# Sums of squares in array quadrants, two tiles at once, and modulation units gathered in rows of one PSUM region

## The chip, the cores and the metric

The kernel runs on one core of one Trainium2 chip, in one launch. The metric is the device time of an execution in microseconds; the lower, the better. TensorE is called PE here, ScalarE ACT, VectorE DVE, GpSimd POOL and SyncE SP.

## What is computed

A stack of three mixer blocks over 512 tokens of width 1024, all in float32. What matters here, cut from the reference:

```python
def _rms(x, gain):
    xf = x.astype(jnp.float32)
    return xf * lax.rsqrt(jnp.mean(xf * xf, axis=-1, keepdims=True) + EPS) * gain.astype(jnp.float32)

def _l2norm(x):
    return x * lax.rsqrt(jnp.sum(x * x, axis=-1, keepdims=True) + EPS)
...
        mod = c_act @ w_ada[layer] + b_ada[layer]          # 1024 -> 3072, for two layers
        shift, scale, gate = mod[:, :D], mod[:, D:2 * D], mod[:, 2 * D:]
...
            mkv = c_act @ w_ada_kv + b_ada_kv              # 1024 -> 2048
...
    q = _l2norm(qkv[..., :W].reshape(B, T, H, Dh)) * (Dh ** -0.5)      # first mixer (GDN), 8 heads of 128
    k = _l2norm(qkv[..., W:2 * W].reshape(B, T, H, Dh))
...
    q = _rms(proj[..., :W].reshape(B, T, H, Dh), q_gain).transpose(0, 2, 1, 3)   # second mixer, 16 heads of 64
...
        q = rms_norm(q.reshape(B, S, N_ATTN_HEADS, HEAD_DIM), q_norm_w) * HEAD_DIM ** -0.5   # third, 24 heads of 64
        k = rms_norm(k.reshape(B, S, N_ATTN_HEADS, HEAD_DIM), k_norm_w)
```

The queries and keys of all three mixers are normalised by the length of each head's vector (128 numbers in the first mixer, 64 in the others), and the modulation is a vector times a matrix, 8192 columns in all.

## The kernel before

Activations lie transposed: the width on the 128 partitions, the 512 tokens along the free axis. One tile is 128 x 512 and holds one head of 128 or two heads of 64. The large products run in blocks of 512 weight columns, two units each (`dense_unit`). ACT splits the raw weights into a high part (`split_hi`, L596), POOL subtracts it to get the low part (`split_lo`, L463), and PE does three products of the parts, 24 matmuls of 512 columns for one tile (L1587). The weights come by SP in loads of 1 MB into two slots of `raw` (L394), freed by POOL's subtraction. Each engine's program is written out by hand in the order in which it runs; semaphores are all that ties the engines together.

**Sums of squares.** For the length of a head ACT squares a tile into one of four `work4` buffers (`square`, L601), and PE multiplies it by a 128 x 128 matrix of ones, `ones` for a head of 128 and `onesbd` (two 64 x 64 blocks of ones) for two heads of 64 (`sums`, L1681). So each of 128 PSUM partitions gets its own head's sum. ACT turns it into a factor in two operations, a Ln out of PSUM (L624) and an Exp in place (L626), in `root`; there are two buffers `rbuf` and two banks, 4 and 5 (`ssbank`). DVE multiplies the tile by the factor (L1145 in GDN, `gained`, L1324, elsewhere) and frees the buffer. PE puts the sums between dense work of the next block: `gdn_sums` in the blocks D_Z and D_Z + 1 of the GDN stage (16 tiles), `head_sums` and `later_sums` elsewhere (40 tiles: KB, QB, QA2, KA2, QB2, KB2, two tiles at a time, with one dense tile between the two pairs that share a unit).

**Modulation units.** The 8192 columns of the modulation are 32 units of 256. A unit is eight matmuls (L1670): the stationary is one column of `cact` repeated 32 times, the moving operand 128 x 256 weights, and four strips of 32 output partitions, k % 4, take the products. The first eight units run at the start. The other 24 are fillers in the first mixer's inverse, one at the head of each pair of heads and one in each of its five levels. DVE copies each unit's row out of PSUM into `arow` (`ada_row`, L1080), and before the next unit PE turns it into two columns of 128 in `modps` with two matmuls of one column (`ada_columns`, L1654). At the end DVE adds the biases (L1239).

**A level of the inverse.** For two heads, PE does 2 x 8 matmuls of 64 x 64 (L1816), a filler, then 2 x 16 more (L1829, L1831). DVE merges the first product into `yib` in between (`copy_predicated`, L1229), ACT copies the rest out (L741, L743), POOL restores a buffer (L480).

```python
                    for s in range(2):
                        ...
                            last = mm(block64(3 * s + 1, i, c), ntm[rs, s, i, :], xin[rs, s, i, :],
                                      start=True, stop=True)
                        last.then_inc(y_full, 1)
                    filler()
                    for s in range(2):
                        ...
                        pe.wait_ge(yi_done, n)
```

**Other places.** The attention of the second mixer has matmuls on row halves (L1960: 64 of the 128 rows, all columns) and on column halves (L1995: all rows, 64 columns), and the scan's first products lie on opposite quadrants (L1879). V tiles of the third mixer are copied by ACT (`v_tile`, L949) and moved into place by SP (`v_moves`, L414); the z values of the first two mixers are silu's that ACT takes from PSUM (L685 and L686, L874).

## Time and profile before

| What | us |
|---|---|
| median of 3 runs | 1387.74 (1384.92 to 1388.86) |
| the profiled execution | 1383.2 |
| its span, first to last instruction | 1381.2 |
| PE busy | 1277.0 |
| ACT busy | 551.5 |
| DVE busy | 462.0 |
| POOL busy | 392.1 |
| mean granted clock of PE | 0.959 of full |

The time of an execution is a little more than the span of its instructions, 2.0 us in the profiled one. Busy times add up the instructions of an engine; an engine that is busy for most of the span is a candidate for the bound, and a stage is bound by the engine that others wait for there. In the timelines a float32 matmul shows as two records, so a row "x4" is two matmuls; its start is exact, and its end overlaps the start of the next, so costs are read from start to start. The times in brackets are how long the engine had been idle and who released it.

### The profile page before, as it was taken

Reading aid. Unit: us, or ns where it says so; the run is one execution under the profiler, and the core shown is the slowest. Engines: PE = TensorE matmul, PEld = TensorE weight load, DVE = VectorE, ACT = ScalarE, POOL = GpSimd, SP = SyncE. Lnnn points to the kernel's source line nnn. Section 1 sums busy time; section 2 is a strip of 40 time slices with the busy share of each in tenths; the row PEclk is TensorE's granted clock in tenths of the full one; section 3 lists DMA queues with packets and bytes.
Section 4 is the critical chain, followed back from the end, with each engine's and each line's share of the span. In section 5 each row is a group of like instructions: output and inputs, shape, how many; then the busy total and the mean of one; then the engine's idle time right before and its main releaser. Section 6 shows DMA issues by size and latency. Waiting matters only on the chain.

```text
span 1381.2 us, 20140 instructions
## 1 busy us (share of the span) xinstructions
PE 1277.0 (92%) x8386; PEld 976.4 (71%) x8386; DVE 462.0 (33%) x852; ACT 551.5 (40%) x926; POOL 392.1 (28%) x170
## 2 busy tenths in 40 slices
PE   5699999889989798999997887989999999999979
PEld 3488876677878676777774554867887777777647
DVE  0665533333234314242213334130202332323441
ACT  4244348522224423343345774233233433644400
POOL 0244432222234331333440001224143222335131
PEclk9799999999999899999999999999999999998969
DMA  9533321155550111222222000132132321224001
GB/s 302 155 92 91 91 92 61 50 167 168 171 185 1 62 61 61 92 91 92 82 77 63 19 20 31 62 97 89 34 107 92 99 69 62 72 85 172 9 0 61
DMA packets 106571, 120.48 MB, mean 87 GB/s; under 512 B 5072, under 2 KB 92528, under 8 KB 106488
## 3 DMA queue, kind: packets, MB, share of 16 engines
q1 hardware_dynamic: 102224, 114.83, 26.0%
q10 hardware_dynamic: 4264, 4.45, 1.1%
q8 instruction: 63, 1.03, 0.3%
q14 instruction: 20, 0.16, 0.0%
HBM read 111.41 MB, written 2.10 MB: 82 GB/s over the span
## 4 chain that ended last, share of the span: by engine, by line
PE 82%; ACT 8%; DVE 4%; issue 3%; DMA 2%; SPq 1%; ACTq 0%; POOL 0%; DVEq 0%
PE ps L1587 47%; PE ps L1681 4%; PE ps L2120 3%; PE ps L1960 2%; PE ps L1670 2%; PE ps L1831 2%; PE ps L1977 2%; PE ps L1829 2%; PE ps L1995 1%; PE ps L2089 1%; PE ps L1902 1%; PE ps L2076 1%; PE ps L1897 1%; PE ps L1816 1%; PE ps L2036 1%
## 5 line engine op out<-in xcount | busy, mean ns | idle before, releaser
L463 POOL TENSOR_TENSOR wlo<-raw,whi 128x2048 fp32r<-128x2048 f32 x58 | 266.6, 4597 | 685.0 <-ACT whi L596 541.1
L596 ACT ACTIVATE whi<-raw 128x2048 fp32r<-128x2048 f32 x56 | 106.9, 1911 | 268.9 <-PE ps L1587 234.3
L1681 PE MATMUL ps<-work,cs 128*128 128x512 f32 x160 | 77.9, 607 | 4.3 <-ACT work L601 4.1
L624 ACT ACTIVATE rbuf<-ps,cs 128x512 f32<-128x512 f32 x59 | 40.0, 678 | 63.7 <-PE ps L1681 49.0
L471 POOL TENSOR_TENSOR wlo<-raw,whi 128x2048 fp32r<-128x2048 f32 x10 | 46.2, 4621 | 66.9 <-ACT whi L660 66.9
L983 ACT ACTIVATE p<-sc,nmx 128x256 f32<-128x256 f32 x64 | 32.0, 502 | 59.0 <-DVE nmx L1428 59.0
L1587 PE MATMUL ps<-hC_hi,whi 128*128 128x512 f32 x208 | 55.3, 408 | 0.0
L1587 PE MATMUL ps<-hC_lo,whi 128*128 128x512 f32 x208 | 51.4, 389 | 0.0
L1587 PE MATMUL ps<-hC_hi,wlo 128*128 128x512 f32 x208 | 51.4, 389 | 0.0
L660 ACT ACTIVATE whi<-raw 128x2048 fp32r<-128x2048 f32 x12 | 23.0, 1920 | 68.7 <-PE ps L1587 63.4
L1681 PEld LDWEIGHTS ps<-work,cs 128*128 128x128 f32 x160 | 29.6, 192 | 29.1 <-issue 17.3
L1359 DVE SCALAR_TENSOR_TENSOR nlk<-ps,att 128x768 f32<-128x768 f32 x16 | 15.3, 958 | 98.1 <-ACT att L896 98.1
L1587 PEld LDWEIGHTS ps<-hC_hi,whi 128*128 128x128 f32 x208 | 38.9, 188 | 12.2 <-issue 4.6
L1977 PE MATMUL ps<-nlk,cs 128*128 128x128 f32 (+3 forms) x128 | 44.8, 453 | 1.7 <-DVE nlk L1359 1.7
L1587 PEld LDWEIGHTS ps<-hC_lo,whi 128*128 128x128 f32 x208 | 39.0, 188 | 8.3
L1587 PEld LDWEIGHTS ps<-hC_hi,wlo 128*128 128x128 f32 x208 | 39.0, 188 | 8.1
L1428 DVE CUSTOM_DVE_ANT_0 sc<-ps,biast 128x256 f32<-128x256 f32 (+1 forms) x64 | 23.6, 398 | 62.6 <-PE ps L2067 32.9
L1587 PE MATMUL ps<-hA_hi,whi 128*128 128x512 f32 x176 | 43.5, 389 | 0.0
L1587 PE MATMUL ps<-hA_lo,whi 128*128 128x512 f32 x176 | 43.5, 389 | 0.0
L1587 PE MATMUL ps<-hA_hi,wlo 128*128 128x512 f32 x176 | 43.5, 389 | 0.0
L741 ACT ACTIVATE xin<-ps 128x128 f32<-128x128 f32 x32 | 9.0, 281 | 84.9 <-PE ps L1831 84.9
L1960 PE MATMUL ps<-qTb,kTb 64*128 64x512 f32 (+1 forms) x64 | 27.4, 551 | 15.7 <-ACT att L900 12.7
(369 smaller groups left out, 2867.9 us busy)
## 6 DMA issues: line engine op xcount, KB each, us to landing
raw<-in_w_in_dram SPq DMA_DIRECT2D x24, 1024.0 KB, 5.1
raw<-in_w_in_a_dram SPq DMA_DIRECT2D x16, 1024.0 KB, 5.5
raw<-in_w_ada_dram SPq DMA_DIRECT2D x16, 1024.0 KB, 5.1
raw<-in_w_ada_kv_dram SPq DMA_DIRECT2D x8, 1024.0 KB, 5.3
raw<-in_w_kv_dram SPq DMA_DIRECT2D x8, 1024.0 KB, 5.2
raw<-in_w_in_b_dram SPq DMA_DIRECT2D x8, 1024.0 KB, 5.2
ada_a<-in_w_ada_dram SPq DMA_DIRECT2D x4, 1024.0 KB, 9.1
ada_b<-in_w_ada_dram SPq DMA_DIRECT2D x4, 1024.0 KB, 12.6
```

What stands on the lines that cost most here:

```text
L463: pool.tensor_tensor(wlo[:, s, :], raw[:, s, :], whi[:, s, :].bitcast(F32), ALU.subtract).then_inc(lo_ready, 1)
L471: pool.tensor_tensor(wlo[:, s, :], raw[:, s, :], whi[:, s, :].bitcast(F32), ALU.subtract).then_inc(lo_ready, 1)
L596: A(whi[:, s, :], raw[:, s, :], ACT.Copy).then_inc(hi_ready, 1)
L624: A(rbuf[:, g % 2, :], ssbank(g), ACT.Ln, scale=1.0 / width, bias=epsc).then_inc(ss_read, 1)
L983: A(p2[:, n % 2, 256 * e:256 * e + 256], sc2[:, n % 2, 256 * e:256 * e + 256], ACT.Exp, scale=-1.0, bias=nmx[:, grp, t, 2 * hp + e:2 * hp ...
L1587: last = mm(out, l[a], r[b], start=start and at == 0, stop=stop and at == n - 1)
L1670: last = mm(modrow(u)[32 * (k % 4):32 * (k % 4) + 32, :], cact[:, k:k + 1].broadcast_to([128, 32]), src[:, k, :], start=k < 4, stop=k >= 4)
L1681: mm(ssbank(g), stat, work4[:, n % 4, :], start=first, stop=last).then_inc(sq_used, 1)
L1829: mm(block64(3 * s + 2, i, c), XT[rs, h, i, :], yib[rs, s, lv % 2, i, :], start=True, stop=True)
L1960: last = mm(logit_cols(s, off[j], 512 - 128 * j), k, q, start=j != 3, stop=True, skip_group_check=True)
L1977: last = mm(logit_cols(s, off[j], width), C("negtri"), nlk[s][:, off[j]:off[j] + width], start=False, stop=True, skip_group_check=True)
L2120: last = mm(dense[2 * s + m], w[:, k, 128 * m:128 * m + 128], x[:, k, :], start=q == 0, stop=q == 23)
```

## The change

It does four things.

1. `head_sums` takes two tiles together. Each is summed in two matmuls of a 64 x 64 block of ones: the first tile's halves go to their own partitions, the second tile's halves to each other's. The four matmuls use the four quadrants of the array, in the order up-up, up-down, down-down, down-up (rows used, then partitions written).
2. `gdn_sums` takes two tiles together as well, with 128 x 64 ones: one tile's sum is written to partitions 0 to 63 and the other's to 64 to 127 of one bank (`gdn_bank`).
3. On ACT `root_pair` and `root_halves` take the place of two calls of `root`. The first has three Ln (the second tile's halves are put back to their partitions) and two Exp; the second has one Ln for both tiles and four Exp on 64 partitions, two for each tile, since both halves of its 128 partitions need the same sums.
4. The 24 later modulation units no longer use a repeated column: the stationary is a window of 32 columns of `cactz`, zero but for one column, so that unit n adds only to row n of each strip, and all 24 gather in one PSUM region. One copy by DVE and two matmuls (`late_columns`) turn all of them into columns at the end; `ada_columns` and `ada_row` are gone from the loop. POOL builds `cactz` once.

```diff
+                cactz = sb("cactz", [128, KD, 55], F32, s2)
...
+        def gdn_bank(g):
+            return ps[:, 4 + (g - G_GDN) // 2 % 2, :]
...
+            pool.wait_ge(hlo_ready, KD)
+            pool.memset(cactz[:, :, :], 0.0).then_inc(cz_done, 1)
+            pool.wait_ge(cz_done, 1)
+            pool.wait_ge(cact_ready, 1)
+            pool.tensor_copy(cactz[:, :, 23:24], cact[:, :].unsqueeze(2)).then_inc(cz_done, 1)
...
+            def root_pair(g, summed):
+
+                act.wait_ge(sq_used, summed)
+                r_used(g - 1)
+                first, second = rbuf[:, g % 2, :], rbuf[:, (g + 1) % 2, :]
+                A(first, ssbank(g), ACT.Ln, scale=1.0 / 64, bias=epsc).then_inc(ss_read, 1)
+                A(second[0:64, :], ssbank(g + 1)[64:128, :], ACT.Ln, scale=1.0 / 64, bias=epsc[64:128, :])
+                A(second[64:128, :], ssbank(g + 1)[0:64, :], ACT.Ln, scale=1.0 / 64, bias=epsc[0:64, :]).then_inc(ss_read, 1)
+                act.wait_ge(ss_read, g + 1)
+                A(first, first, ACT.Exp, scale=-0.5).then_inc(r_ready, 1)
+                act.wait_ge(ss_read, g + 2)
+                A(second, second, ACT.Exp, scale=-0.5).then_inc(r_ready, 1)
+
+            def root_halves(g, summed):
+
+                act.wait_ge(sq_used, summed)
+                r_used(g - 1)
+                first, second = rbuf[:, g % 2, :], rbuf[:, (g + 1) % 2, :]
+                A(second, gdn_bank(g), ACT.Ln, bias=epsc).then_inc(ss_read, 2)
+                act.wait_ge(ss_read, g + 2)
+                A(first[64:128, :], second[0:64, :], ACT.Exp, scale=-0.5)
+                A(first[0:64, :], second[0:64, :], ACT.Exp, scale=-0.5).then_inc(r_ready, 1)
+                act.wait_ge(r_ready, g + 1)
+                A(second[0:64, :], second[64:128, :], ACT.Exp, scale=-0.5).then_inc(rh_read, 1)
+                act.wait_ge(rh_read, (g - G_GDN) // 2 + 1)
+                A(second[64:128, :], second[64:128, :], ACT.Exp, scale=-0.5).then_inc(r_ready, 1)
...
-                for t in range(t0, t0 + 4):
-                    root(G_GDN + t, SQ_GDN + t + 1, 1)
+                for t in (t0, t0 + 2):
+                    root_halves(G_GDN + t, SQ_GDN + t + 2)
...
-                filler_row()
...
-                    filler_row()
-
-
-            while rows_left:
-                ada_row(rows_left.pop(0))
-            dve.wait_ge(mod_full, 32)
-            TT(mods[:, 16:64], modps[:, 16:64], cols1[:, 40:88], ALU.add).then_inc(mods_ready, 1)
+
+            dve.wait_ge(ada_done, 32)
+            copy(arow[:, 0, :], modrow(2 * EARLY)).then_inc(row_done, 1)
+            dve.wait_ge(mod_full, 2 * EARLY + 1)
+            TT(mods[:, 16:64].rearrange("p (u m) -> p m u", m=2), modps[:, 16:64].rearrange("p (m u) -> p m u", m=2),
+               cols1[:, 40:88].rearrange("p (u m) -> p m u", m=2), ALU.add).then_inc(mods_ready, 1)
...
+            def late_columns():
+
+                pe.wait_ge(row_done, 2 * EARLY + 1)
+                for m in range(2):
+                    last = mm(modps[:, 16 + 24 * m:40 + 24 * m], arow[:, 0, 128 * m:128 * m + 128], C("sel32"),
+                              start=True, stop=True)
+                last.then_inc(mod_full, 1)
+
+            def late_unit(a, s):
+
+                n = 2 * (a - EARLY) + s
+                pe.wait_ge(raw_loaded[s], 16 * (load_of["ada", a] + 1))
+                if n == 0:
+                    pe.wait_ge(cz_done, 2)
+                for k in range(KD):
+                    last = mm(modrow(2 * EARLY)[32 * (k % 4):32 * (k % 4) + 32, :], cactz[:, k, 23 - n:55 - n],
+                              raw_ch(s)[:, k, :], start=n == 0 and k < 4, stop=n == 23 and k >= 4, skip_group_check=True)
+                last.then_inc(ada_done, 1)
...
-            def head_sums(n0, g0):
-                for j in range(2):
-                    sums(n0 + j, g0 + j, onesbd)
+            def head_sums(n, g):
+
+                pe.wait_ge(sq_ready, n + 2)
+                pe.wait_ge(ss_read, g)
+                up, down = slice(0, 64), slice(64, 128)
+                for tile, of, to in ((0, up, up), (1, up, down), (0, down, down), (1, down, up)):
+                    last = mm(ssbank(g + tile)[to, :], ones[of, 0:64], work4[of, (n + tile) % 4, :], start=True, stop=True)
+                last.then_inc(sq_used, 2)
...
             def gdn_sums(*tiles):
-                for t in tiles:
-                    sums(SQ_GDN + t, G_GDN + t, ones)
+                if not tiles:
+                    return
+                n, g = SQ_GDN + tiles[0], G_GDN + tiles[0]
+                pe.wait_ge(sq_ready, n + 2)
+                if tiles[0] >= 4:
+                    pe.wait_ge(ss_read, g - 2)
+                for k in range(2):
+                    last = mm(gdn_bank(g)[64 * k:64 * k + 64, :], ones[:, 0:64], work4[:, (n + k) % 4, :],
+                              start=True, stop=True)
+                last.then_inc(sq_used, 2)
```

The order moves in three kinds of place; all the dense work stays where it was.

PE, one level of the inverse of the first pair of heads, before (xin and ntm are the level's operands, cs and arow the constants and the row that is turned, raw and cact the weights and the activated vector):

```order
L1816 MATMUL ps<-xin,ntm 64x64 x16
L1654 MATMUL ps<-cs,arow 128x1 x2
L1670 MATMUL ps<-raw,cact 32x256 x8
L1829 MATMUL ps<-yib,xa 64x64
L1831 MATMUL ps<-xa,yib 64x64
```

and in the changed kernel:

```order
L1874 MATMUL ps<-xin,ntm 64x64 x16
L1705 MATMUL ps<-raw,cactz 32x256 x8
L1887 MATMUL ps<-yib,xa 64x64
L1889 MATMUL ps<-xa,yib 64x64
```

The two matmuls of one column are gone; the eight of the unit now stand right behind the sixteen of the level.

PE, the first two pairs of head sums (tiles KB of the keys, in the blocks D_KB + 1), before:

```order
L1587 MATMUL ps<-hk_hi,wlo 128x512 x8
L1681 MATMUL ps<-work,cs 128x512 x2
L1587 MATMUL ps<-hk_hi,whi 128x512 x8
L1587 MATMUL ps<-hk_lo,whi 128x512 x8
L1587 MATMUL ps<-hk_hi,wlo 128x512 x8
L1681 MATMUL ps<-work,cs 128x512 x2
```

and in the changed kernel:

```order
L1619 MATMUL ps<-hk_hi,wlo 128x512 x8
L1738 MATMUL ps<-work,cs 64x512 x4
L1619 MATMUL ps<-hk_hi,whi 128x512 x8
L1619 MATMUL ps<-hk_lo,whi 128x512 x8
L1619 MATMUL ps<-hk_hi,wlo 128x512 x8
L1738 MATMUL ps<-work,cs 64x512 x4
```

Two matmuls of 128 columns of weights became four of 64, at the same places.

ACT, the first pair of roots of the KB tiles, before:

```order
L601 ACTIVATE work<-kTb 128x512 x2
L596 ACTIVATE whi<-raw 128x2048
L624 ACTIVATE rbuf<-ps,cs 128x512
L626 ACTIVATE rbuf<-rbuf 128x512
L624 ACTIVATE rbuf<-ps,cs 128x512
L626 ACTIVATE rbuf<-rbuf 128x512
```

and in the changed kernel:

```order
L614 ACTIVATE work<-kTb 128x512 x2
L609 ACTIVATE whi<-raw 128x2048
L646 ACTIVATE rbuf<-ps,cs 128x512
L647 ACTIVATE rbuf<-ps,cs 64x512
L648 ACTIVATE rbuf<-ps,cs 64x512
L650 ACTIVATE rbuf<-rbuf 128x512
L652 ACTIVATE rbuf<-rbuf 128x512
```

Ln and Exp used to alternate; now three Ln stand ahead of two Exp. In GDN the first pair of roots is, in the changed kernel:

```order
L614 ACTIVATE work<-qkvT 128x512 x4
L659 ACTIVATE rbuf<-ps,cs 128x512
L661 ACTIVATE rbuf<-rbuf 64x512
L662 ACTIVATE rbuf<-rbuf 64x512
L664 ACTIVATE rbuf<-rbuf 64x512
L666 ACTIVATE rbuf<-rbuf 64x512
```

where before stood:

```order
L601 ACTIVATE work<-qkvT 128x512 x4
L624 ACTIVATE rbuf<-ps,cs 128x512
L626 ACTIVATE rbuf<-rbuf 128x512
L624 ACTIVATE rbuf<-ps,cs 128x512
L626 ACTIVATE rbuf<-rbuf 128x512
```

One Ln and four Exp on 64 partitions are in the place of two Ln and two Exp.

## Rows read from the trace of the kernel before

**Rows 1.** The page: busy time by engine; granted clock and DMA rate in 40 slices

```profile
PE 1277.0 (92%) x8386; PEld 976.4 (71%) x8386; DVE 462.0 (33%) x852; ACT 551.5 (40%) x926; POOL 392.1 (28%) x170
...
PEclk9799999999999899999999999999999999998969
...
GB/s 302 155 92 91 91 92 61 50 167 168 171 185 1 62 61 61 92 91 92 82 77 63 19 20 31 62 97 89 34 107 92 99 69 62 72 85 172 9 0 61
```

**Rows 2.** The page: shares of the chain of waits by engine

```profile
PE 82%; ACT 8%; DVE 4%; issue 3%; DMA 2%; SPq 1%; ACTq 0%; POOL 0%; DVEq 0%
```

**Rows 3.** Timeline of PE, 1177 to 1186 (start, duration, line, operation, records)

```profile
1177.26 1.88 PE L1681 MATMUL ps<-work,cs 128*128 128x512 f32 x4
...
1182.65 1.98 PE L1587 MATMUL ps<-hC_hi,wlo 128*128 128x512 f32 x8
1184.46 1.88 PE L1681 MATMUL ps<-work,cs 128*128 128x512 f32 x4
```

**Rows 4.** Timeline of PE in the attention, 799 to 804

```profile
799.58 2.37 PE L1995 MATMUL ps<-att,Vb 128*64 128x512 f32 x16
801.88 0.69 PE L1960 MATMUL ps<-qTb,kTb 64*128 64x512 f32 x1
...
803.37 0.40 PE L1963 MATMUL ps<-bandbf 128*128 128x128 bf16 x4
```

**Rows 5.** Timeline of PE, one level of the inverse, 280 to 286

```profile
280.90 1.43 PE L1816 MATMUL ps<-xin,ntm 64*64 64x64 f32 x32
282.26 0.61 PE L1654 MATMUL ps<-cs,arow 128*128 128x1 f32 x4
282.79 1.07 PE L1670 MATMUL ps<-raw,cact 128*32 128x256 f32 x16
283.79 0.34 PE L1829 MATMUL ps<-yib,xa 64*64 64x64 f32 x4
...
285.71 1.43 PE L1816 MATMUL ps<-xin,ntm 64*64 64x64 f32 x32
```

**Rows 6.** Timeline of PE, start of the scan

```profile
411.30 1.96 PE L1879 MATMUL ps<-V,xa 64*64 64x128 f32 x32 [0.39 <-DVE mods L1239]
```

**Rows 7.** Timeline of ACT in the GDN stage, roots and z values

```profile
219.95 0.69 ACT L624 ACTIVATE rbuf<-ps,cs 128x512 f32<-128x512 f32 x1 [1.03 <-DVE qkvT L1145]
...
221.20 0.67 ACT L624 ACTIVATE rbuf<-ps,cs 128x512 f32<-128x512 f32 x1
...
223.85 0.59 ACT L685 ACTIVATE zs<-ps 64x512 f32<-64x512 f32 x1
```

**Rows 8.** Timeline of ACT, first gate values of the z block

```profile
703.07 1.57 ACT L874 ACTIVATE zsT<-ps 128x512 f32<-128x512 f32 x3
```

**Rows 9.** Tile vB, its moves and their landing; timeline of PE there

```profile
L414 SPq DMA_DIRECT2D vB<-yst x8: 594/596/1290, 1258.4 to 1263.7; - x8
...
DMA to landing us min/median/max: 2.0/2.1/3.1
...
1266.44 1.12 PE L2089 MATMUL ps<-pT,vB 128*64 128x128 f32 x8
```

**Rows 10.** Timeline of PE at 306; windows (busy us, count; clock, DMA share, GB/s)

```profile
306.12 0.68 PE L1816 MATMUL ps<-xin,ntm 64*64 64x64 f32 x16 [1.25 <-DVE xin L1222]
...
297.50:320.00 22.50, 19.90 (x384) 17.08 (x383) 9.83 (x29) 7.35 (x24) 4.12 (x6) 0.92 0.42 132
```

**Rows 11.** Timeline of DVE in the level of rows 5

```profile
282.37 0.29 DVE L1229 COPY_PREDICATED yib<-cs,ps 128x128 f32<-128x128 int32 x1 [0.46 <-PE ps L1816]
```

**Rows 12.** Timelines of PE and ACT, the waits of the GDN stage

```profile
214.20 1.98 PE L1681 MATMUL ps<-work,cs 128*128 128x512 f32 x4 [1.37 <-ACT work L601]
...
232.52 1.98 PE L1681 MATMUL ps<-work,cs 128*128 128x512 f32 x4
...
231.84 2.19 ACT L601 ACTIVATE work<-qkvT 128x512 f32<-128x512 f32 x4
...
257.45 1.16 PE L1789 MATMUL ps<-cs,gt 128*128 128x128 f32 x8 [0.42 <-ACT zs L686]
```

More of the change, by code:

```diff
@@ L67, in constants @@
     put("first32", p % 32 == 0)
+    put("sel32", p % 32 == np.arange(24)[None, :])
     def dft(n):
@@ L830, in row_squares, with roots @@
                         square(sq + j, src(j))
-            def roots(g, sq, js=range(4)):
+            def roots(g, sq, js=(0, 2)):
                 for j in js:
-                    root(g + j, sq + j + 1, 64)
+                    root_pair(g + j, sq + j + 2)
             def copies(d, dst, done, func):
@@ L1763, in filler @@
                 if fill:
-                    ada_unit(*fill.pop(0))
+                    late_unit(*fill.pop(0))
             for p in range(HG // 2):
```

31 lines of the change are left out of this document (12 added, 19 removed).

## The prediction

> **What bounds the kernel now.** I read the page first, by engine and by slice: TensorE (PE) is busy 92% of the 1381.2 us, and the granted clock is close to full nearly everywhere [rows 1]. The chain that ended last lies 82% on PE [rows 2]. So a microsecond taken off PE is a microsecond of the span wherever PE has no waits, and nothing where it waits. Hence the order of views: the timeline of PE around each place that the change touches, then the timelines of ACT, DVE and the SP queue at the same moments, to see who would be late next.
>
> **The change, part by part.**
>
> *Head sums (20 pairs of tiles: KB 4, QB 4, QA2 2, KA2 2, QB2 4, KB2 4).* Today a pair is two matmuls with a 128x128 stationary and 512 columns (each is two records in the trace). From the start of one pair to that of the next there are 7.20 us, with one dense tile between [rows 3]. That tile is 24 matmuls, three groups of 8, and the last group takes 1.81 us (1184.46 less 1182.65), so 5.44 us in all. A pair costs 7.20 - 5.44 = 1.76 us, 0.88 us for one matmul. Afterwards a pair is four 64x64 matmuls of 512 columns, one in each quadrant of the array. Before has no four quadrants at once, so bounds: not under 0.88 us, since each still streams 512 columns; 1.76 us if they run two at a time; 3.5 us if one at a time. The nearest rows are these. In the attention, 16 records (8 matmuls, 2560 columns, alternating between two column halves) run from 799.58 to 801.88, that is 2.30 us where 2560 columns at 0.88 per 512 would take 4.40 [rows 4]: two of 512 columns at once cost 0.92 us. In the modulation units eight matmuls of 256 columns in four column strips take 1.00 us [rows 5] where one after another would take 3.52. Ideal would be 0.88, so 0.12 us is for weights and for leaving and entering the shape. Rows and columns of the array can therefore be shared by neighbours: strips share all rows, and matmuls on the two row halves, which share all columns, take 1.49 us for 1280 columns (801.88 to 803.37; 2.20 one by one) [rows 4]. I take 1.00 us for a pair: 0.76 saved, 20 times, 15.2 us.
>
> The Trainium skill (PSUM — Partial Sum Buffer, section on bank collisions) says that different row tiles cannot access the same PSUM bank at the same time. Here both halves of a bank are written from different row halves, so by that rule at most two of the four would overlap. The trace leans the other way: 32 records (16 matmuls of 128 columns) whose neighbours sit on opposite row halves and write opposite halves of one bank take 1.96 us, where 16 x 128 columns at 0.88 per 512 would be 3.52 [rows 6]. They overlap, in one bank. By the rule the 15.2 us would be about nothing; it stays a rival.
>
> What covers the ACT side. root_pair has five ACT operations for four, the two new ones on 64 partitions, and 64 partitions cost as much as 128 (0.59 us, [rows 7]). But the two Ln of the second tile now stand between a Ln and its Exp, and fill the bubble there; a pair goes from 2 x 1.25 us [rows 7] to some 2.7. In the dense stages ACT idles 3 us and more before each pair (3.60 us is the usual), so 0.2 us is hidden; without that idle it would be 4 us over 20 pairs. Two places give something back. Behind the last pair of QB, ACT's first gate value of the z block is done at 703.07 + 0.60 = 703.7 [rows 8], and PE, one dense tile behind that pair, comes to its bank at 704.8; PE will be 1.5 us earlier there: -0.3. Behind the last pair of KB2 the V tiles are copied by ACT and moved by SP (32 DMAs of 0.6 us). The last is issued at 1263.7 and lands 2.1 us later, 1265.8, and PE's first weighted sum starts at 1266.44 [rows 9]. The start of these moves hangs on ACT's last pair, whose start is set by DVE's use of the roots before it, which a subtraction on POOL holds up. So they don't get earlier, and of PE's last 1.5 us only some 0.3 remain: -1.2. Head sums: 15.2 - 0.3 - 1.2 = **13.7 us**.
>
> *Modulation units.* Between the levels of the inverse, PE does a filler: two matmuls that turn the previous row into columns (L1654), then eight for the next unit (L1670). In the steady pattern L1816 starts at 280.90, L1654 at 282.26, L1670 at 282.79, L1829 at 283.79, L1816 again at 285.71 [rows 5]: no wait, a period of 4.81 us of which L1654 takes 0.53. The change removes it 23 times, and keeps one pair at the end. Three of the 23 stand at the head of a later pair of heads, ahead of a 1.25 us wait for DVE [rows 10]: worth nothing, since DVE's chain does not shorten. The other 20 are worth 0.53 each, one of them 0.95 (the first level of all, at the low clock): **11.0 us**. Who is late next? L1829 waits for DVE's merge, which ends 0.40 us after L1816 (282.37 + 0.29 = 282.66, [rows 11]); the eight matmuls left, 1.00 us, still cover it. If they did not, up to 0.4 us a level would be lost. The stationary of a unit is now 32 different columns instead of one repeated, at the same shape; I cost that at nothing. The 24 copies of rows on DVE (0.42 us each) go too; DVE was not the bound. The loads of 1 MB are still released by the units; a period of 4.28 us asks for 245 GB/s instead of 218, and the first slice of the page shows 302 [rows 1], so I expect no wait. POOL's new memset and copy fall in a 21 us idle stretch of POOL.
>
> *GDN sums (8 pairs).* On PE the same gain, 0.76 x 8 = 6.1 us. But ACT sets the pace here. PE waits 1.37 us for ACT's squares at 214.20, finds them just ready at 232.52, and waits 0.42 us for zs at 257.45 [rows 12]. root_halves has one Ln and four Exp on 64 partitions, three of them chained by semaphores: about 0.72 + 0.55 + 3 x 0.62 = 3.1 us, for 2.5 [rows 7]. And PE now waits for both squares of a pair, 0.54 us more. At the first wait: ACT 0.1 later and both squares needed, so PE starts its pair 0.7 later and finishes it as before. By the second wait ACT has done two longer pairs, so its squares (231.84) start 1.1 later, PE begins at 234.1 instead of 232.52 and is 0.8 us behind. Three more pairs make it 1.5 ahead, but then ACT's last pair is 0.6 longer, and the zs values come only some 0.2 us earlier. PE just waits longer at 257.45. GDN: **0.2 us**, between -3 (ACT's 8 x 0.6 all on the path, less what PE gains at the ends) and +1.5.
>
> Sum: 13.7 + 11.0 + 0.2 = 24.9 us. The profiled execution took 1383.2 us, so it would be 1358.3. The median of the runs is 4.5 us above it, 1387.7, so the forecast is **1362.8 us**.
>
> **Rivals.**
> A. *Two quadrants at a time* (the PSUM rule above, or a limit of another kind on four streams). A pair costs 1.76 + 0.12 = 1.9 us, the head sums lose 2.8 us, and the total is 11.0 + 0.2 - 2.8 = 8.4: 1379.3 us. For it: no row shows four quadrants. Against it: rows 6, and the four strips of rows 5. Chance 0.12.
> B. *Quadrants that share a row or a column half do not overlap.* In the order issued (up-up, up-down, down-down, down-up) each neighbour shares a side, so all four run one by one: 3.5 + 0.1 = 3.6 us, 1.84 more than now, 20 times, 36.8 us on a bound PE. Total +36.8 - 11.0 - 0.2 = +25.6: 1413.3 us, slower. It decides as soon as a pair costs over 2.3 us. Against it: strips share rows, row halves share columns, and both overlap [rows 4, 5]; but none does it at 64x64. Chance 0.06.
> C. *The levels do not get shorter.* With less work between DVE's waits the clock stays low for longer: today it is 0.92 over 297.5 to 320 us, which holds such a start [rows 10], and the first level there runs at half rate. Were one more level at half rate in each of the four head pairs (about 2.4 us each), or were the DMAs to set the period, most of the 11 us would go: 1373 us. Chance 0.10.
> That the two parts do not do what they say is covered by A and B for the sums. For the units the instructions removed are plain in the order.
>
> **How the numbers follow.** Forecast 0.70 (1358 to 1370: pair cost 0.88 to 1.2, GDN -3 to +1.5, levels 9 to 12), A 0.12, B 0.06, C 0.10, and 0.02 for about no change by waits that I have not seen. The range takes in C and reaches to A: 1358 to 1378. About 0.3% (4 us) is what a measurement can tell from no change, and A and C are past that too: faster 0.70 + 0.12 + 0.10, less 0.02 for their edge, 0.90; same 0.04; slower 0.06.
>
> **What would show it.** A pair of head sums at about 1.0 us, 6.4 us from one to the next in the KB2 stage; under 0.9 or over 1.3 the sizing is wrong, at 1.9 it is A, at 3.6 B. No 128x1 matmuls in the levels, and a period of 4.28 us; a wait on DVE before the 64x64 matmuls behind the filler, or on the raw loads, would be C. In GDN longer waits of PE for the squares at about 212 and 232 us and for zs at about 256. A wait of about 1 us before the first weighted sum of the second window, on the V moves. If the head stages shrink by less than 12 us while the pair costs 1.0, ACT's five operations were not hidden after all.

## The result, and the profile after

The changed kernel took **1367.1 us** (median of 4 runs, 1365.0 to 1371.8), the kernel before beside it 1388.0: ratio 0.986, 95% interval 0.983 to 0.989. That is 20.9 us less, where 24.9 was forecast and 1362.8 us named. The profiled execution of the change is its slowest, 1371.8 us with a span of 1369.7; the one of before was among its fastest, 1383.2. In a later comparison (e9 below), the change took 1367.7 against 1388.4.

The page after, lines that answer to [rows 1, 2]. The shares of the chain add up to 82% here and to 100% before: as the view follows it, this chain begins only at 236 us, so 68% does not mean that PE counts for less.

```profile
PE 1257.0 (92%) x8374; PEld 950.5 (69%) x8374; DVE 439.5 (32%) x829; ACT 570.0 (42%) x954; POOL 393.8 (29%) x172
...
PEclk9799998999999899999998999999999999999969
...
GB/s 302 160 93 92 92 92 33 55 163 193 179 186 1 62 62 61 93 92 93 92 98 34 20 20 4 77 84 89 62 94 78 129 41 87 66 88 181 9 1 62
```

```profile
PE 68%; ACT 8%; issue 3%; DVE 3%; POOL 0%; DMA 0%; SPq 0%; ACTq 0%; DVEq 0%
```

PE is 20 us less busy and just as full in proportion; ACT is 18 us busier (570.0 for 551.5). So in most places the time went with PE's work, as it should where PE is the bound. The slices of the page are too coarse to say where not. I cut both traces at the first product of each stage in PE's timeline instead:

| stage (from, to: first product of) | before | after |
|---|---|---|
| start to the first GDN sum | 200.38 | 199.42 |
| GDN sums, to the first head of the inverse (L1789, now L1847) | 57.07 | 62.53 |
| inverse, with the modulation units, to the scan | 153.85 | 143.44 |
| scan, first part (to the first transposed output) | 26.09 | 26.09 |
| rest of the scan, KB and QB (8 pairs of head sums) | 292.87 | 289.87 |
| attention, to the first product of the third mixer's wfs | 212.76 | 216.99 |
| QA2 and KA2 (4 pairs) | 140.36 | 138.69 |
| first window, QB2 and KB2 (8 pairs) | 177.05 | 173.10 |
| second window | 58.38 | 57.06 |
| end, to PE's last product | 59.19 | 59.39 |

The inverse gave what was forecast, the head sums two thirds of it, and GDN lost 5.5 us where 0.2 were to be gained. Three views show how.

**A pair of head sums.** PE's timeline in KB of the changed kernel (start, duration, line, operation, records), which answers to [rows 3]:

```profile
564.72 1.09 PE L1738 MATMUL ps<-work,cs 64*64 64x512 f32 x8
565.74 2.11 PE L1619 MATMUL ps<-hk_hi,whi 128*128 128x512 f32 x8
567.69 1.99 PE L1619 MATMUL ps<-hk_lo,whi 128*128 128x512 f32 x8
569.52 1.98 PE L1619 MATMUL ps<-hk_hi,wlo 128*128 128x512 f32 x8
571.42 1.09 PE L1738 MATMUL ps<-work,cs 64*64 64x512 f32 x8
```

From its own start to that of the next work a pair takes 1.02 us (565.74 less 564.72): four quadrants do run at once. But the next pair starts 6.70 us later, not 6.4. The dense tile in between takes 5.68 and not the 5.44 of three groups at 1.81: its first group takes 1.95 and its last 1.90, the middle one 1.83. By the forecast's own sum a pair costs 6.70 - 5.44 = **1.26 us**.

The pair's 1.02 us must not be set against the same cut in the kernel before. There, in the period of [rows 3],

```profile
1178.57 2.42 PE L1587 MATMUL ps<-hC_hi,whi 128*128 128x512 f32 x8
```

follows 1.31 us behind the start of the pair (1177.26), and the dense tile then takes 5.89. The first dense record starts 0.03 us after the last record of the sums, though one such record takes 0.43. So part of the sums' time lies behind that start, and only whole periods, 7.20 and 6.70, can be compared.

**A level of the inverse**, in PE's timeline, which answers to [rows 5]:

```profile
314.00 1.44 PE L1874 MATMUL ps<-xin,ntm 64*64 64x64 f32 x32
315.37 1.07 PE L1705 MATMUL ps<-raw,cactz 128*32 128x256 f32 x16
316.37 0.34 PE L1887 MATMUL ps<-yib,xa 64*64 64x64 f32 x4
...
318.28 1.43 PE L1874 MATMUL ps<-xin,ntm 64*64 64x64 f32 x32
```

The period is 4.28 us, and nothing waits for DVE.

**The GDN sums**, in PE's timeline, which answer to [rows 12]; in brackets how long PE stood idle and for whom:

```profile
209.39 1.07 PE L1619 MATMUL ps<-whi,hA_lo 128*128 128x512 f32 x4
214.54 1.98 PE L1788 MATMUL ps<-work,cs 128*64 128x512 f32 x4 [4.08 <-ACT work L614]
216.44 2.08 PE L1619 MATMUL ps<-whi,hA_hi 128*128 128x512 f32 x4
...
220.98 1.08 PE L1788 MATMUL ps<-work,cs 128*64 128x512 f32 x4
...
236.11 1.21 PE L1788 MATMUL ps<-work,cs 128*64 128x512 f32 x4 [1.96 <-ACT work L614]
```

The wait of 1.37 us has become 4.08, and one of 1.96 is new; both stand where the forecast had longer waits, and are longer than it had them. What follows the waits is slow: the pair at 214.54 takes 1.90 us to the next start where the one at 220.98 takes 1.01. The window of this stage, of both kernels (busy PE and count, granted clock, DMA share, GB/s), first after:

```profile
199.42:261.95 62.53, 54.84 (x221) 0.92 0.11 37
```

In the kernel before, with the other engines' busy time ahead of the clock (PE, PEld, DVE, ACT, POOL):

```profile
200.38:257.45 57.07, 55.28 (x222) 37.10 (x220) 15.17 (x29) 43.46 (x73) 10.31 (x6) 1.00 0.13 41
```

The clock was full all through before. Now it falls to its lower level, 1.2 GHz, at both idles: 0.51 of full from 212.9 to 219.9, 0.52 from 236.8 to 240.3, and 1.00 in the rest of the stage. ACT's own timeline shows what comes ahead of the squares:

```profile
200.59 0.69 ACT L659 ACTIVATE rbuf<-ps,cs 128x512 f32<-128x512 f32 x1 [4.14 <-issue]
201.31 0.63 ACT L661 ACTIVATE rbuf<-rbuf 64x512 f32<-64x512 f32 x1
...
203.28 0.63 ACT L666 ACTIVATE rbuf<-rbuf 64x512 f32<-64x512 f32 x1
208.19 0.69 ACT L659 ACTIVATE rbuf<-ps,cs 128x512 f32<-128x512 f32 x1 [4.29 <-DVE qkvT L1185]
...
213.35 2.17 ACT L614 ACTIVATE work<-qkvT 128x512 f32<-128x512 f32 x4
```

A pair of roots takes 3.3 us (200.59 to 203.91) instead of 2.5. The second pair waits 4.29 us for DVE to use the first roots, and DVE stands at its copy of the gate products (L1179), which wait for PE. Only then come the split and the squares for which PE waits at 214.54. That wait is not new. The kernel before has it at the same place, and longer:

```profile
209.23 0.69 ACT L624 ACTIVATE rbuf<-ps,cs 128x512 f32<-128x512 f32 x1 [5.21 <-DVE qkvT L1145]
...
213.53 2.17 ACT L601 ACTIVATE work<-qkvT 128x512 f32<-128x512 f32 x4
```

What the change did to it shows when times are counted from the first GDN sum (200.38 before, 199.42 after), before and after: DVE's copy starts at 7.48 and 6.78, ACT's second roots at 8.85 and 8.77, its squares at 13.15 and 13.93, PE's pair at 13.82 and 15.12. The copy comes 0.70 us earlier, since PE gained that much, but the roots gain next to nothing from it: a pair of them needs both buffers back, so it waits for two scalings of DVE (0.6 us each) where one was enough. Then the roots take 0.8 longer, and PE waits for two squares and not one. PE itself is there 1.4 us earlier, and that too is in the 4.08.

### The profile page after: what moved, and what is told of

The parts are those of the page before. It is cut to its first block, busy times and chain, and to the rows that moved or that the text cites. A ratio compares the mean times of both kernels' runs of the same rounds, so it can differ in the third digit from the quotient of the medians.

```text
span 1369.7 us, 20045 instructions
## 1 busy us (share of the span) xinstructions
PE 1257.0 (92%) x8374; PEld 950.5 (69%) x8374; DVE 439.5 (32%) x829; ACT 570.0 (42%) x954; POOL 393.8 (29%) x172
## 4 chain that ended last, share of the span: by engine, by line
PE 68%; ACT 8%; issue 3%; DVE 3%; POOL 0%; DMA 0%; SPq 0%; ACTq 0%; DVEq 0%
PE ps L1619 36%; PE ps L2178 3%; PE ps L2035 2%; PE ps L2018 2%; PE ps L1705 2%; PE ps L1889 2%; PE ps L1887 1%; PE ps L2053 1%; PE ps L1738 1%; PE ps L1960 1%; PE ps L2147 1%; PE ps L1955 1%; PE ps L1874 1%; PE ps L2094 1%; PE ps L2134 1%
## 5 line engine op out<-in xcount | busy, mean ns | idle before, releaser
L2035 PE MATMUL ps<-nlk,cs 128*128 128x128 f32 (+3 forms) x128 | 48.5, 485 | 2.8 <-DVE nlk L1391 2.8
L1328 DVE SCALAR_TENSOR_TENSOR xT<-ps,mods,xT 128x512 f32<-128x512 f32 x16 | 12.0, 751 | 89.7 <-PE ps L1619 89.7
L2018 PE MATMUL ps<-qTb,kTb 64*128 64x512 f32 (+1 forms) x64 | 26.0, 528 | 15.6 <-ACT att L940 12.6
L1874 PE MATMUL ps<-xin,ntm 64*64 64x64 f32 x640 | 27.8, 224 | 13.4 <-DVE xin L1256 11.9
L1889 PE MATMUL ps<-xa,yib 64*64 64x64 f32 x640 | 38.8, 226 | 0.0
```

What stands on the lines that cost most here:

```text
L1889: last = mm(block64(3 * s, i, c), yib[rs, s, lv % 2, i, :], XT[rs, h, i, :], start=True, stop=True)
L2018: last = mm(logit_cols(s, off[j], 512 - 128 * j), k, q, start=j != 3, stop=True, skip_group_check=True)
L2035: last = mm(logit_cols(s, off[j], width), C("negtri"), nlk[s][:, off[j]:off[j] + width], start=False, stop=True, skip_group_check=True)
```

## The experiments

Twelve runs, in three groups (e1 to e4, e5 to e8, e9 to e12), each group beside the kernel before on one chip; the medians of the kernel before there are 1387.3, 1385.7 and 1388.4 us. Three things were open: how the three parts add up, why GDN loses, and why a pair costs 1.26 us.

### The parts one by one: e1, e2, e3, e4

Each kernel is the change with some parts put back as before. e1 keeps the modulation units alone, e2 the head sums, e3 the GDN sums, e4 both head sums and units. Against the change, e4 is:

```diff
-                for t in (t0, t0 + 2):
-                    root_halves(G_GDN + t, SQ_GDN + t + 2)
+                for t in range(t0, t0 + 4):
+                    root(G_GDN + t, SQ_GDN + t + 1, 1)
...
-                for k in range(2):
-                    last = mm(gdn_bank(g)[64 * k:64 * k + 64, :], ones[:, 0:64], work4[:, (n + k) % 4, :],
-                              start=True, stop=True)
-                last.then_inc(sq_used, 2)
+                for t in tiles:
+                    sums(SQ_GDN + t, G_GDN + t, ones)
```

> The modulation part of the change alone; head and GDN sums of squares as before. Theory (the parts are independent, the term was right): in the profile of the changed kernel a level repeats every 4.28 us, where before it was 4.81, and the stretch from the first inverse to the scan was 10.4 us shorter. So 10 to 11 us under the kernel before, about 1377.5, with a level period of 4.28 us and the scan's start 10 us earlier. Rival (the levels were shorter only because another part of the change helped, or part of the gain is given back by the attention): 4 to 8 us.

> The four-quadrant head sums alone (with their paired roots on ScalarE); modulation and GDN sums as before. The recorded term said 0.76 us a pair, 13.7 us in all. Theory now, from the changed kernel's profile: the four products take 1.02 us, but from one pair to the next 6.70 us pass and not the 6.4 forecast, since the dense products on both sides of it take some 0.26 us longer than 8 of them elsewhere; so 0.50 us a pair, 20 pairs 10.0 us, less 0.3 at the z block and 1.2 before the second window: 8 to 9 us under the kernel before, about 1379.5. Rival (the term was right and the 0.26 us are this profile's own): 13 to 14 us.

> The GDN part alone: sums of two tiles in halves of one bank, five ScalarE operations a pair of tiles; head sums and modulation as before. The recorded term said 0.2 us gained, with -3 (slower) to +1.5. Theory now: slower by 4 to 6 us, about 1393, since TensorE waits some 4 us and 2 us for squares and the granted clock falls to 1.2 GHz behind each wait (the changed kernel's stretch from the first GDN sum to the first head sum was 5.5 us longer). Rival: the stretch belongs to that one execution, or the modulation part took TensorE work from it; then within 1.5 us of the kernel before.

> The change without its GDN part. Theory: 4 to 6 us under the changed kernel and 24 to 26 under the kernel before if the GDN part costs 5.5 us everywhere, about 1363; the sum of the two single parts (10.5 and 8.5) would give 19, about 1369, and then the GDN part costs nothing in the median. The stretch from the first GDN sum to the first head sum goes back to some 57 us, with the granted clock at 1.00 in it.

Measured, with the stages cut as above. "rest of scan" is the stage of 8 pairs; the 12 pairs stand in "QA2, KA2" and "first window".

| | us, median | ratio, 95% | GDN | inverse | scan, first part | rest of scan | attention | QA2, KA2 | first window |
|---|---|---|---|---|---|---|---|---|---|
| before | 1387.3 | | 57.07 | 153.85 | 26.09 | 292.87 | 212.76 | 140.36 | 177.05 |
| e1 units | 1371.7 | 0.990 (0.987 to 0.993) | 57.07 | 145.38 | 33.34 | 293.42 | 212.80 | 140.39 | 177.18 |
| e2 heads | 1373.9 | 0.991 (0.989 to 0.993) | 57.07 | 156.40 | 26.10 | 290.02 | 210.42 | 138.56 | 173.05 |
| e3 GDN | 1389.7 | 1.002 (1.000 to 1.004) | 62.36 | 154.74 | 32.41 | 293.43 | 216.10 | 140.39 | 177.16 |
| e4 heads, units | 1364.0 | 0.982 (0.980 to 0.985) | 57.09 | 145.10 | 33.48 | 289.90 | 211.21 | 138.60 | 173.13 |

In the GDN stage and the first window each part does its own work and no other: the one is 57.07 or 62.4, the other 177.1 or 173.1, each to 0.2 us, by its own part alone. So the GDN part costs 5.3 us in its stage, units or no units, and the rival that the stretch belonged to one execution falls. The whole of e3 was expected 4 to 6 us slower; its median is only 2.4 above the kernel before, and its interval reaches from 0.6 to 6.0 us. e2 confirms 0.50 us a pair where pairs follow closely (first window, 4.0 us for 8), and its rival, 13 to 14 us, is not what the rows show, though the median (12.5 us by the ratio) lies nearer to it. The medians of e1 and e2 are 4 to 5 us better than the rows of their parts. One stage shows how large such luck is. The first part of the scan has no part of the change in it, and takes 26.1 us or 33.4. Windows of e4's and of before's scan (busy PE, granted clock):

```profile
403.06:436.54 33.48, 33.48 (x289) 0.76 0.01 1
```

```profile
411.30:437.39 26.09, 26.09 (x288) 1.00 0.01 1
```

PE is busy all through in both; in e4's first 15.9 us, to 419.0, the granted clock was 0.50. Such draws sit in the inverse and in the attention too. I take them to be why a single execution of one kernel differs from the next by 7 us and more, and trust the stages over the medians for terms of a few microseconds.

### The low clock in GDN: e5

Products that nobody reads are put in front of the two long waits; nothing else of the change differs.

```diff
+                for _ in range({4: 5, 8: 3}.get(tiles[0], 0)):
+                    mm(ps[:, 7, :], ones, cs[:, 0:512], start=True, stop=True)
```

> The changed kernel with 5 and 3 products (128x128 by 128x512, into a bank that nobody reads then) added in front of TensorE's two long waits in the GDN part (4.08 us at 214.54 and 1.96 at 236.11), nothing else. Theory: the waits are ScalarE's and stay as long in all, but TensorE is busy through them, so the granted clock stays at 1.00 and the two stretches behind them, that took 1.90 + 4.6 and 1.2 + 4.45 us where the same work takes 1.01 + 2.9 at full clock, give back some 4.3 us: first GDN sum to first head sum 58.2 us instead of 62.5, and about 4 us under the changed kernel. Rival (ScalarE alone sets the stretch, so TensorE's faster work only waits longer): the stretch stays at 62 us or more, and the time within 1 us of the changed kernel's, or above it by the added products.

PE's timeline of e5 there, and its window (PE, PEld, DVE, ACT, POOL busy, clock):

```profile
210.07 4.45 PE L1785 MATMUL ps<-cs 128*128 128x512 f32 x10
214.46 1.08 PE L1790 MATMUL ps<-work,cs 128*64 128x512 f32 x4
215.47 1.20 PE L1619 MATMUL ps<-whi,hA_hi 128*128 128x512 f32 x4
```

```profile
199.18:258.66 59.48, 57.67 (x238) 35.44 (x237) 15.26 (x29) 49.20 (x81) 12.62 (x13) 1.00 0.12 39
```

The pair comes at the same moment, 214.46 for 214.54, and takes 1.01 us instead of 1.90. The stage is 59.5 us, 3.0 less than in the change, with the clock at 1.00. The theory said 58.2: its 4.3 us was the cost of the slow work. Behind the first wait PE now needs 3.95 us to its next pair of sums, 2.5 less than in the change, but there it waits for ACT again, and the pair after that wait comes only 1.5 us earlier in the stage (35.2 for 36.7). Behind the second wait another 1.5 us is gained. So of the 5.5 us lost in GDN, **3.0 are the clock**. The 2.4 that are left at full clock are the longer waits, less what PE saved in its sums. The whole kernel did not get faster (1370.3 us, ratio 0.988, 0.984 to 0.991): its profile has the inverse at 146.1 us against 143.4 in the change's. That miss is one of the draws above, or something that I can't tell from one.

### What a pair costs: e6 and e7

Both are e4 with one line changed: e6 issues the four products twice (the same sums, written twice), e7 in an order in which no neighbours read the same rows.

```diff
-                for tile, of, to in ((0, up, up), (1, up, down), (0, down, down), (1, down, up)):
+                for tile, of, to in 2 * ((0, up, up), (1, up, down), (0, down, down), (1, down, up)):
...
+                for tile, of, to in ((0, up, up), (0, down, down), (1, up, down), (1, down, up)):
```

> The changed kernel without its GDN part (e4), with every pair's four quadrant products issued twice over (the same sums, written twice). It asks what a pair costs by itself: the second four cost only their own work, and what the change of tile shape costs is paid once, as in e4. Theory (1.26 us a pair is 0.9 to 1.0 of work and some 0.3 of shape change): a pair to the next goes from 6.70 to 7.6 us, and the whole 17 to 20 us above e4, about 1382. Rival (the 1.26 us are work alone, the shape change costs nothing): 7.96 us from pair to pair and 25 us above e4. If quadrants waited for one another it would be more.

> The changed kernel without its GDN part (e4), with the four quadrant products of a pair in another order: first the two that read a tile's own half and write it (up to up, down to down), then the two crossed ones, so that no neighbours share rows. Theory (four quadrants run side by side whatever their order, and two of them writing one bank costs nothing): pair 1.02 us, 6.70 from pair to pair, and e4's time within 1 us. Rival (neighbours that share neither rows nor columns start earlier, or the shape change is cheaper): a pair to the next under 6.6 us and the time 2 to 4 us under e4. Rival (the order in the change was chosen because crossing order matters to the banks): over 6.9 us and 4 us above.

e6, PE's timeline in KB2:

```profile
1180.18 1.95 PE L1738 MATMUL ps<-work,cs 64*64 64x512 f32 x16
1182.06 2.11 PE L1619 MATMUL ps<-hC_hi,whi 128*128 128x512 f32 x8
1184.00 1.98 PE L1619 MATMUL ps<-hC_lo,whi 128*128 128x512 f32 x8
1185.81 1.98 PE L1619 MATMUL ps<-hC_hi,wlo 128*128 128x512 f32 x8
1187.72 1.95 PE L1738 MATMUL ps<-work,cs 64*64 64x512 f32 x16
```

From pair to pair 7.54 us: the second four add 0.84 (7.54 less 6.70), less than the 0.88 of one full product before. So the four share the array without loss, the rival's 7.96 us falls, and 1.26 - 0.84 = **0.42 us** is paid once for each excursion from the 128x128 shape to the 64x64 one and back, 0.24 of it in the dense groups next to the pair. The sums differ from the dense work in more than the shape, as they aren't split into parts; but so they did before, at 128x128, where four records at 0.43 us make 1.71 of the 1.76 us of a pair. At most 0.05 us of the 0.42 is left for that. (The kernel took 1385.0 us, 21 above e4 on another chip; in the stages the 20 pairs cost 15.6 more.) In e7:

```profile
1175.16 1.09 PE L1738 MATMUL ps<-work,cs 64*64 64x512 f32 x8
1176.18 2.11 PE L1619 MATMUL ps<-hC_hi,whi 128*128 128x512 f32 x8
...
1181.86 1.09 PE L1738 MATMUL ps<-work,cs 64*64 64x512 f32 x8
```

Again 1.02 and 6.70 us: the order is worth nothing, and both its rivals fall. Its 1369.4 us lie 5 above e4, which its stages don't bear out: they agree with e4's to 0.2 us but for the attention, 0.9 us shorter, and the end, 0.6 longer.

### GDN in another order: e8, and e12

The whole change, with as much arithmetic, in an order that takes DVE's copy out of ACT's way. PE sums both pairs of four tiles one behind the other, before the gate products and not around them, and DVE scales two tiles before it copies the gate products. `gates_and_four` holds the gates' transposes and then tiles 4 to 7, both behind the first dense tile.

```diff
-            dve.wait_ge(ba_full, 1)
-            copy(bat[:, :], ps[0:16, 6, :]).then_inc(bat_done, 1)
...
-            lengths(0, 4)
+            lengths(0, 2)
+            dve.wait_ge(ba_full, 1)
+            copy(bat[:, :], ps[0:16, 6, :]).then_inc(bat_done, 1)
+            lengths(2, 4)
...
             gdn_sums(0, 1)
+            gdn_sums(2, 3)
...
+            def gdn_four(at, t0):
+                def beside(t):
+                    if t == at:
+                        gdn_sums(t0, t0 + 1)
+                        gdn_sums(t0 + 2, t0 + 3)
+                return beside
...
-            dense_unit(D_Z, 1, hA, lambda t: gdn_sums(*((4, 5), (6, 7), ())[t]))
+            dense_unit(D_Z, 1, hA, gates_and_four)
...
-            dense_unit(D_Z + 1, 0, hA, lambda t: gdn_sums(*((), (8, 9), (10, 11))[t]))
-            dense_unit(D_Z + 1, 1, hA, lambda t: gdn_sums(*((12, 13), (14, 15), ())[t]))
+            dense_unit(D_Z + 1, 0, hA, gdn_four(2, 8))
+            dense_unit(D_Z + 1, 1, hA, gdn_four(1, 12))
```

> The changed kernel with another order in the GDN part, and as much arithmetic: the two pairs of each four tiles are summed one behind the other, (2, 3) before the gate products and not behind them, (8 to 11) and (12 to 15) at the places where their squares are there; on VectorE the copy of the gate products stands behind the first two scalings and no longer ahead of them; the gates' transposes one dense tile later. Theory: what made TensorE wait 4.08 us was ScalarE, held 4.3 us at 208.19 by VectorE, whose first scaling stood behind that copy, and then by a chain of roots, split and squares. With both gone ScalarE comes to the squares of 4 to 7 at 209 instead of 213.3, TensorE waits no more than 1 us at any place, the clock stays at 1.00, and the stretch from the first GDN sum to the first head sum goes from 62.5 to 53 to 56 us: 7 to 9 us under the changed kernel, about 1359, and 2 to 5 us under e4. Rival (ScalarE's five operations a pair fill the stretch, whatever their order): 60 us or more, and the changed kernel's time.

e8, the timelines of ACT and then of PE:

```profile
203.05 0.69 ACT L659 ACTIVATE rbuf<-ps,cs 128x512 f32<-128x512 f32 x1 [0.84 <-DVE qkvT L1182]
...
208.21 2.17 ACT L614 ACTIVATE work<-qkvT 128x512 f32<-128x512 f32 x4
```

```profile
209.39 2.12 PE L1788 MATMUL ps<-work,cs 128*64 128x512 f32 x8 [0.97 <-ACT work L614]
...
229.54 1.94 PE L1788 MATMUL ps<-work,cs 128*64 128x512 f32 x8
231.40 1.21 PE L1619 MATMUL ps<-whi,hA_hi 128*128 128x512 f32 x4
...
251.03 0.66 PE L1846 MATMUL ps<-cs,qkvT 128*128 128x128 f32 x4 [3.56 <-ACT zs L726]
```

ACT's wait for DVE went from 4.29 to 0.84 us, its squares come at 208.2 instead of 213.4, PE waits 0.97 us for them and not 4.08, and the second wait is gone. The stage takes 55.8 us, at the upper end of the 53 to 56 expected and 6.8 under the change's. So ACT's five operations need not cost the stage anything against the 57.1 before, if the queues are ordered for them, and the rival of 60 us or more falls. It does not follow that their order caused the loss: the kernel before has the same order and the same wait of ACT (5.21 us), and e8 takes that away as well. What this order would give with the sums one by one was not run. The whole kernel took 1359.9 us (ratio 0.983, 0.980 to 0.987), 7.3 under the first result of the change, on another chip. Two pairs at once take 1.86 us to the next start, one pair 1.01: the second is cheaper here too, as the fixed part is paid once. What is left is at the end, 3.56 us for ACT's z values, where no wait over 1 us had been expected, and e12 tests that. In it the last four tiles are summed one by one as before (`sums`, `root`).

> As e8, but tiles 12 to 15 summed one by one as before the change (all partitions, four ScalarE operations for two tiles and not five). In e8 TensorE's largest wait left in the stretch is 3.56 us at 251.03 for ScalarE's z silu. Theory (ScalarE ends the stretch there): ScalarE's roots get 2 x 0.8 us shorter, TensorE's sums 4 x 0.88 - 1.9 = 1.6 us longer inside its wait, so the stretch goes from 55.8 to some 54.2 us and the time 1 to 2 us under e11. Rival (DMA or TensorE sets the end): the same time, or 1 to 2 us more.

That stage takes 53.2 us, one more off than expected, and 2.6 less than with pairs there (e8). PE no longer waits before its first transposes; only 0.50 us is left ahead of the next products:

```profile
241.49 4.22 PE L1730 MATMUL ps<-work,cs 128*128 128x512 f32 x8
...
251.05 0.60 PE L1854 MATMUL ps<-cs,qkvT 128*128 128x128 f32 x4
...
252.62 1.16 PE L1867 MATMUL ps<-cs,gt 128*128 128x128 f32 x8 [0.50 <-ACT zs L730]
```

### Side by side: e9, e10, e11

The change, e4 and e8 once more, with e12 on one chip.

> The changed kernel once more, beside the next three on one chip, since its executions lie up to 8 us apart and the comparison so far was of few. Theory: 1367 to 1369, its stretch from the first GDN sum to the first head sum 62.5 us, and single executions fall into groups some 7 us apart, by whether the granted clock is 0.5 or 1.0 in the first 14 us of the scan. Rival (the first comparison took it too slow): 1363, the forecast.

> The change without its GDN part once more, on the same chip. Theory: 3 to 6 us under the changed kernel beside it (its stretch was 5.4 us shorter, 57.1). Rival (a later wait or the clock gives it back): within 1.5 us of it.

> The kernel with four tiles' GDN sums at once (e8) on the same chip. Theory: 6 to 9 us under the changed kernel beside it and 1 to 4 under the one without the GDN part, as its stretch was 55.8 us against 62.5 and 57.1. Rival: the same as the one without the GDN part, since ScalarE's longer chain gives back what TensorE gains.

| | us, median of 6 | lowest, highest | ratio to before, 95% | GDN stage, first and second profile |
|---|---|---|---|---|
| e9 the change | 1367.7 | 1362.5, 1376.6 | 0.986 (0.983 to 0.990) | 62.53, 62.60 |
| e10 without its GDN part | 1367.0 | 1362.8, 1372.2 | 0.986 (0.983 to 0.989) | 57.09, 57.07 |
| e11 four at once | 1366.3 | 1355.5, 1368.4 | 0.984 (0.981 to 0.987) | 55.76, 55.79 |
| e12 last four alone | 1364.8 | 1354.4, 1368.8 | 0.983 (0.979 to 0.986) | 53.20 |

The stage repeats to 0.1 us, and the order of the medians is the order of the stages. But the differences are smaller than expected: e10 0.7 us under e9 where 3 to 6 were, e11 1.4 where 6 to 9 were. By these runs none of the four is told from another. Over all executions of the comparisons (10 of the change, 12 of e4 and e10, 12 of e8 and e11) the means are 1368.1, 1365.6 and 1363.4, in the expected order, with half to two thirds of the expected steps. **A GDN part without loss is shown for its stage; for the whole kernel it is likely, and what it is worth is not settled** (1.4 us by e11 beside e9, 7.3 by e8 against the first result). e12 has the lowest median of the four and the shortest stage; I would take it, knowing that.

## Why the prediction was right, and where it was off

**Modulation units, 11.0 forecast: right.** The inverse took 153.9, 156.4 and 154.7 us in the three profiles without the new units (before, e2, e3), 155.0 in the mean, and 140.5 to 147.6, 144.3 in the mean, in the other eleven: 10.7 us. The stage's length follows its granted clock, and at an equal one the gain is the forecast: 156.4 us in e2 and 145.4 in e1, both at 0.924, 11.0 apart. The period is 4.28 us as forecast, and in it no load or DVE came late. Rival C would have needed one more level at half clock for each pair of heads; by the mean that did not come.

**Head sums, 13.7 forecast: the mechanism right, the pair mis-sized.** Four quadrants run at once (1.02 us as forecast 1.00), A and B fall. The Trainium skill (PSUM — Partial Sum Buffer, section on bank collisions) has different row tiles unable to access one bank at the same time; in this kernel two row halves write opposite partition halves of one bank, and the four take 0.84 us where one full product takes 0.88. The measurement decides. The step that failed is "0.12 us is for weights and for leaving and entering the shape". I had measured that from rows inside small-shape work, and took what lies around a pair to be the unchanged 5.44 us of a dense tile. It is 5.68, and the excursion costs 0.42 us in all. So 0.50 us a pair and not 0.76. In the stages: 3.4 us for 8 pairs in the rest of the scan (293.2 in the mean of before, e1 and e3, 289.9 in the change), 1.7 for 4, 4.0 for 8, **9.1 us**.

ACT's side was mis-sized too. A pair of roots takes 3.2 us (1216.73 to 1219.98), where some 2.7 was forecast. The forecast's own sign for ACT not being hidden, head stages that shrink by less than 12 us with a pair at 1.0, did come. But the excursion is most of it: PE waits for ACT at three pairs only, those that stand half a tile behind the one before and find the split ahead of the roots in ACT's queue, 0.16 us each (as at 593.21). From start to start they save 0.28 us and not 0.50, some 0.7 us in all.

The wait for the V moves came as well: from the second window's first product to its first weighted sum there are 7.43 us (1250.13 to 1257.56), 6.01 before, where 1.2 more was forecast. It cost the window nothing that shows. With the units alone (e1) the window takes 57.1 us, with units and head sums (e4) 57.2; with neither (before) 58.4, with the head sums alone (e2) 58.4. The eleven profiles with the units have 57.1 to 57.6 and e3, the third without them, 57.9. So the 1.3 us that the window got shorter seem to go with the units. The clock does not explain them: it was 0.910 in e2's window and 0.872 in e1's. What does, these runs leave open.

**GDN, +0.2 forecast, -3 to +1.5 as its range: wrong, -5.5.** The step was "PE starts its pair 0.7 later and finishes it as before". The pair started 1.3 later, at 15.12 us of the stage for 13.82. Two things were missing. First, I moved ACT's chain by its own durations alone, and had its squares 0.1 us later; they were 0.8 later. With pairs, ACT needs both buffers back before it goes on. The copy of DVE ahead of that came 0.7 earlier, but a second scaling took it back, and the roots were 0.8 longer where I had 0.6. This repeats: at full clock (e5) the pair behind the second wait starts 3.0 us later than before, where I had 1.6. Second, I priced a longer wait as the wait alone. These two idles of PE, in a stage that ran at full clock, cost another 3.0 us in the work behind them (e5).

**The whole.** The rows give 10.7 + 9.1 - 5.5 = 14.3 us, and 1.3 in the second window, 15.6, where the medians give 20.9 and 20.6. That leaves out the attention, which the change does not touch and which is 4.2 us longer in the change's profile; with it the sum is 11.4, the difference of the two profiled executions.

With 45 executions of before in the later comparisons, the time goes with the mean granted clock, by about 1 us for each 0.001. At 0.963 to 0.964 before took 1379.0 to 1382.5 and the change 1364.2 to 1365.0, some 16 us less, which is what the rows say. Against a straight line through the 45, the change's ten executions lie 17.1 us lower, e1's 11.2 and e2's 8.4 lower, and e3's 2.9 higher, each with an error under 1 us. The three parts add up, to 16.7 us for the 17.1 of the whole. This measure leaves out the clock that a change itself loses, and e3's 2.9 is near the 2.4 that e5 left for GDN at full clock. It also puts the 12 executions of e8 and e11 at 21.8, 4.7 below the change, and those of e4 and e10 at 17.9.

So of the 20.9 us some 16 to 17 are work taken away. The plain means, 1386.1 for the 45 and 1368.1 for the ten, are 18.0 apart; the rest is which executions the medians fell on. The forecast came within 4.3 us partly by that luck: the rows are 9.3 us short of its 24.9.

**Range and chances.** 1367.1 lies inside 1358 to 1378, near the middle. The likeliest case was 1358 to 1370, and came true by its total, with two of its three parts outside their own bounds: a pair cost 1.26 us, not 0.88 to 1.2, and GDN -5.5, not -3 to +1.5.

## What to carry to other kernels

Where a change makes steps coarser (two tiles a step for one), walk through every buffer's hand-over around the loop, queue by queue: how many buffers must be back before the next double step, and what stands ahead of the last return. Look in the kernel before for the wait that you are about to blame; ours was there, and 0.9 us longer. Price a new idle of PE at its length plus what runs at half rate behind it. And price an excursion into another tile shape by what comes before and after it, from the start of one to the start of the next: it pays to do several small-shape products in one go.

## What the hardware showed that I had not expected

- An excursion from 128x128 to 64x64 products and back costs 0.42 us beside the products, about half a full 512-column product (6.70 from pair to pair; 7.54 with the products doubled).
- Keeping PE busy through a wait with products that nobody reads shortened the stage by 3.0 us (62.5 to 59.5), though the first pair behind them came no earlier.
- The scan's first part, busy throughout, takes 26.1 us in eight of the fourteen profiles, 27.3 in one and 32.4 to 33.5 in five, by whether the granted clock is at 1.00 or near 0.5 in its first 14 to 16 us.
- The attention, the same code in all, takes 217.0 us in the five profiles that have the whole change (with e5, e8, e9 and e11), 216.1 in e3, and 210.4 to 211.2 in e4, e7 and e10; but e6, without the GDN part too, has 217.1, and e12 213.7. Its length goes with the granted clock in it: 0.929 where it takes 217.0 and 217.1, 0.945 at 212.8 (before, e1), 0.960 or 0.968 at 211.2 and 210.4. What sets that clock, and whether the GDN part has to do with it, is open; if it has, it costs more than its own stage shows.
